# One stage for the sample's attention and the output projection of a two-branch encoder layer

## The reference, cut to what matters

```python
def mixer_layer(x, c, pos, past_sb_k, past_sb_v, past_ckv, past_krope, ...):
    h = rms_norm(x, pre_g) * (1.0 + scale) + shift
    sb_q, sb_k, sb_v, sb_g, c_q, c_kv, k_rope, mla_g = split_cols(h @ w_in, IN_SIZES)
    ...
    sb_o = sweep_query_blocks(stick_breaking_block, (sb_q,), (all_sb_k, all_sb_v), pos, k_pos)
    mla_o = sweep_query_blocks(mla_block, (q_nope, q_rope), (k_nope, all_krope, mla_v), pos, k_pos)
    mixed = jnp.concatenate([sb_o.reshape(b, t, SB_WIDTH) * jax.nn.silu(sb_g),
                             mla_o.reshape(b, t, MLA_WIDTH) * jax.nn.silu(mla_g)], axis=-1)
    y = x + gate * rms_norm(mixed @ w_out, post_g)
```

## Time and profile before

| what | value |
|---|---|
| device time, 3 runs | 2635.29, 2643.12, 2650.52 us; median 2643.12 |
| profiled execution | 2648.48 us device time; span 2646.7 us from first to last instruction |
| busy shares of the span | PE 85%, PEld 71%, DVE 52%, ACT 50%, POOL 29% |
| granted TensorE clock, mean | 0.917 of full |
| prompt attention | ends at 2088 us |
| sample attention and output | 2091.6 to 2646.7 us |
| transfers from 2090 us on | 81.08 MB in 100408 packets, mean 146 GB/s |

### The profile page before, as it was taken

How to read it: one execution, slowest core, us unless ns; L and a number is a source line. 1 busy time by engine, 2 the same in 40 slices (tenths; PEclk the granted TensorE clock), 3 DMA queues, 4 the chain that set the end, 5 groups by cost and what they waited for, 6 DMA issues and landing times. The chain is left out here.

```text
span 2646.7 us, 40141 instructions
## 1 busy us (share of the span) xinstructions
PE 2248.5 (85%) x12099; PEld 1869.0 (71%) x12099; DVE 1381.5 (52%) x2759; ACT 1323.5 (50%) x2852; POOL 776.9 (29%) x773
## 2 busy tenths in 40 slices
PE   6599996999977899498989999999989577775887
PEld 1488885899967677286868677777778356664765
DVE  2223232210137333487878778787878388863332
ACT  1223222211112433388888888888888555542221
POOL 0000000000000000356474737465563345542321
PEclk9799998899989899699999999999999777777989
DMA  8333322222337898733323343332320444426773
GB/s 292 106 101 95 108 83 89 100 80 82 116 92 198 284 310 290 158 67 69 68 66 75 70 91 67 68 82 58 74 54 23 107 136 135 142 67 196 177 185 93
DMA packets 304695, 314.44 MB, mean 119 GB/s; under 512 B 88322, under 2 KB 234765, under 8 KB 299489
## 3 DMA queue, kind: packets, MB, share of 16 engines
q1 hardware_dynamic: 299810, 297.45, 40.9%
q10 hardware_dynamic: 3744, 12.19, 1.2%
q0 software_dynamic: 992, 3.21, 0.3%
HBM read 194.83 MB, written 109.57 MB: 115 GB/s over the span
## 5 line engine op out<-in xcount | busy, mean ns | idle before, releaser
L1243 ACT ACTIVATE pa_whi<-banks 128x512 fp32r<-128x512 f32 (+3 forms) x640 | 346.4, 542 | 98.9 <-PE banks L1468 77.9
L1468 PE MATMUL banks<-ident,pa_p 128*128 128x128 f32 x2176 | 354.9, 279 | 2.2 <-ACT pa_p L1208 2.2
L1451 PE MATMUL banks<-pa_khi,pa_qst 128*128 128x512 f32 (+3 forms) x640 | 262.7, 410 | 103.9 <-DVE pa_p L1307 77.1
L1397 POOL TENSOR_TENSOR pa_wlo<-pa_whole,pa_whi 128x512 fp32r<-128x512 f32 (+2 forms) x240 | 279.2, 1172 | 191.4 <-ACT pa_whole L1248 190.7
L1379 POOL CAST pa_khi<-pa_kraw 128x512 fp32r<-128x512 f32 x64 | 39.1, 611 | 993.4 <-DMA pa_kraw<-scratch_sb_kT 993.4
L1468 PEld LDWEIGHTS banks<-ident,pa_p 128*128 128x128 f32 x2176 | 268.5, 143 | 61.4 <-issue 5.6
L1428 PE MATMUL banks<-pa_whi,pa_vst 128*128 128x512 f32 (+3 forms) x640 | 285.1, 445 | 1.5 <-POOL pa_wlo L1397 1.4
L1307 DVE TENSOR_TENSOR_SCAN pa_p<-banks,pa_p,pa_zero 128x512 f32<-128x512 f32 x192 | 246.3, 1283 | 71.4 <-ACT banks L1201 62.6
L1451 PEld LDWEIGHTS banks<-pa_khi,pa_qst 128*128 128x128 f32 x640 | 125.7, 196 | 184.2 <-DVE pa_p L1307 142.7
L1284 DVE TENSOR_TENSOR pa_wlo<-banks,pa_whi 128x512 fp32r<-128x512 f32 (+3 forms) x400 | 234.7, 587 | 27.0 <-ACT pa_whi L1243 27.0
L1452 PE MATMUL banks<-pa_klo,pa_qst 128*128 128x512 f32 (+3 forms) x640 | 242.6, 379 | 0.0
(11 more groups left out here) (231 smaller groups left out, 5095.6 us busy)
## 6 DMA issues: line engine op xcount, KB each, us to landing
ada<-in_ada_w_dram SPq DMA_DIRECT2D x6, 2048.0 KB, 11.4
scratch_sb_kT<-ke_kT SPq DMA_DIRECT2D x12, 1024.0 KB, 8.9
scratch_mla_kT<-ke_nT SPq DMA_DIRECT2D x12, 1024.0 KB, 5.5
scratch_mla_v<-ke_v SPq DMA_DIRECT2D x12, 1024.0 KB, 5.4
co_hlo<-scratch_hT SPq DMA_DIRECT2D x6, 1408.0 KB, 6.9
scratch_gatesT<-co_gates SPq DMA_DIRECT2D x12, 704.0 KB, 10.7
pr_x<-in_x_prompt_dram SPq DMA_DIRECT2D x16, 512.0 KB, 4.4
scratch_hT<-pr_hT SPq DMA_DIRECT2D x16, 512.0 KB, 5.3
```

Source lines behind the costliest of these rows:

```text
L1243: act.activation(whi[:, t % NW, q0:], bank, ACT.Copy).then_inc(hi_done, 1)
L1397: pool.tensor_tensor(wlo[:, t % NW, q0:], whole[:, t % 4, q0:], raw(whi[:, t % NW, q0:]), ALU.subtract).then_inc(pool_lo, 1)
L1451: pe.matmul(bank, qst[job][:, q], khi[job][:, keys], start=True, stop=False)
L1468: y = pe.transpose(ps[:, NS + t % NTB, x * P:(x + 1) * P], probs[g][x][:, i * P:(i + 1) * P], s["ident"][:])
```

## The change

`sample_attention_phase` and `output_phase` are replaced by one function, `tail_phase`, with one table of slots. Slot t (from -11 to 78) does: score chunk t + 10, transpose and take out chunk t, one quarter of an output tile (12 matmuls: half of the 8 contraction chunks for one half of the 1024 columns), and mix chunk t - 1. 72 chunks and 64 quarters; quarter i is put into slot i * 8 // 7, so slots 7, 15, ... 71 have none. Each engine has a list per slot. The 16 prompt tiles are projected this way; the sample's own tile keeps its gated, split operands in SBUF (`shi`, `slo`) and is projected at the end (`sample_part`, 42 matmuls in slot 72 and 6 after the last job).

Operands are held in rings: keys `klo` (3 chunks, split in place, with 2 of `khi`), rotary keys `krst` (3), values (3), weights (3). A key chunk is loaded when the chunk three before it has been scored. Scores of a stick-breaking job stay in PSUM: the sigmoid is in place there, and the scan reads PSUM and writes `left`. The copy that makes the high part of the values moves from ACT and DVE to POOL for all chunks. The exponentials of a softmax job are issued in three pieces of three chunks (slots 9J - 1, 9J + 1, 9J + 4). The output's square is taken per half tile, PSUM for the output has three banks. `w_out` comes through a ring of three buffers (the tiles `x` and `y`) during slots -10 to -3; its low part is made by DVE and POOL in turn.

The keys stage now stores the rotary keys split: DVE writes `krhi` and `krlo` (one more 32-row subtraction per tile), SP issues three transfers per group in place of one; prompt attention loads the 96 rows in one transfer without splitting them.

```diff
@@ keys_phase
-                    sp.dma_start(d["mla_krT"][:, at], krT[:, b, 0:n]).then_inc(krT_stored[b], 16)
+                    for i, tile in enumerate((krhi, krhi, krlo)):
+                        sp.dma_start(d["mla_krT"][i * ROPE:(i + 1) * ROPE, at], raw(tile[:, b, 0:n])).then_inc(krT_stored[b], 16)
...
-                        dve.tensor_copy(krT[:, b, at], ps[0:ROPE, 2 + j % 2, RC * P:RC * P + rows])
+                        rope = ps[0:ROPE, 2 + j % 2, RC * P:RC * P + rows]
+                        dve.tensor_copy(krhi[:, b, at], rope).then_inc(kr_hi, 1)
...
+                        dve.wait_ge(kr_hi, NT * g + j + 1)
+                        dve.tensor_tensor(krlo[:, b, at], rope, raw(krhi[:, b, at]), ALU.subtract).then_inc(c_ev, 1)
@@ prompt_attention_phase
-                for i in range(3):
-                    sp.dma_start(early[i * ROPE:(i + 1) * ROPE, 0:T], d["mla_krT"][:, 0:T]).then_inc(kr_loaded, 16)
+                sp.dma_start(raw(krst[:]), d["mla_krT"][:, 0:T]).then_inc(kr_loaded, 16)
...
-                act.activation(krst[:], early[0:3 * ROPE, 0:T], ACT.Copy).then_inc(kr_hi, 1)
...
-                dve.tensor_tensor(krst[lo, :], early[lo, 0:T], raw(krst[lo, :]), ALU.subtract).then_inc(const_done, 1)
@@ tail_phase
+    AHEAD = 10
+    RING = 3
+    FIRST_SLOT, END_SLOT = -AHEAD - 1, U + 7
...
+        def quarter_slot(i):
+            return i * 8 // 7
+        def tile_slot(n):
+            return quarter_slot(4 * n)
+        def half_slot(n, i):
+            return quarter_slot(4 * n + 2 * i + 1)
...
+                def load_k(u):
...
+                    if u >= RING:
+                        sp.wait_ge(scores, u - RING + 1)
...
+                    for n in tiles:
+                        if t == tile_slot(n) - 7:
+                            load_tile(n)
+                        if t == tile_slot(n) + 2:
+                            load_x(n)
+                        if t == half_slot(n, 1) + 3:
+                            store(n)
...
+            @block.scalar
+                for t in slots:
...
+                    if 0 <= t + AHEAD < U and not is_soft(t + AHEAD):
+                        sigmoid(t + AHEAD)
+                    for n in tiles:
+                        for i in range(2):
+                            if t == half_slot(n, i) + 1:
+                                square(n, i)
+                    if 0 <= t < U:
+                        high(t)
+                    if 0 <= t + AHEAD + 1 < U:
+                        split_k(t + AHEAD + 1)
+                    for J in range(1, JOBS, 2):
+                        for at, pieces in ((-1, (0, 1, 2)), (1, (3, 4, 5)), (4, (6, 7, 8))):
+                            if t == NCH * J + at:
+                                for k in pieces:
+                                    exp(NCH * J + k)
...
+                        if t == half_slot(n, 1) + 1:
+                            root(n)
...
+            @block.vector
+                    if 0 <= u < U:
+                        if is_soft(u):
+                            cut(u)
+                        else:
+                            scan(u)
+                    if 0 <= t < U:
+                        low(t)
...
+                    if 0 <= u + 1 < U:
+                        split_k(u + 1)
...
+            @block.tensor
+                def score(u):
...
+                    pe.wait_ge(k_split, u + 1)
...
+                    if u >= 2:
+                        pe.wait_ge(cut_done if is_soft(u - 2) else scan_done, nth(u - 2) + 1)
...
+                for t in slots:
+                    if 0 <= t + AHEAD < U:
+                        score(t + AHEAD)
+                    if 0 <= t < U:
+                        turn(t)
...
+                    for i in range(4 * TILES):
+                        if t == quarter_slot(i):
+                            quarter(*divmod(i, 4))
+                    if 0 <= t - 1 < U:
+                        mix(t - 1)
```

More of the change, by code:

```diff
@@ new lines, in tail_phase @@
+        scores, sig_done, scan_done, taken_done = sm.one("scores"), sm.one("sig"), sm.one("scan"), sm.one("taken")
+        cut_done, negtop_done, exp_done = sm.one("cut"), sm.one("negtop"), sm.one("exp")
+        total_done, inverse_done = sm.one("total"), sm.one("inverse")
+        turned, hi_done, lo_done, mix_done = sm.one("turned"), sm.one("hi"), sm.one("lo"), sm.one("mix")
+        half_done, summed, divided, gated, shi_done, slo_done = (
+            sm.one(n) for n in ("half", "summed", "divided", "gated", "shi", "slo"))
@@ L1599, in sample_attention_phase, with columns @@
+        def columns(i):
+            return slice(i * CH, (i + 1) * CH)
+        slots = range(FIRST_SLOT, END_SLOT)
+        tiles = range(TILES)
         with nc.Block() as block:
@@ L1819, in finish, with take_inverse @@
+                def take_inverse(J):
+                    e = entry(NCH * J + NCH - 1) + 1
+                    dve.wait_ge(turned, e + 1)
+                    if J > 1:
+                        dve.wait_ge(divided, J // 2)
                     for hd in range(2):
                         part = slice(hd * HD, (hd + 1) * HD)
[L1821 to L1823 removed]
@@ L1838, in _, with finish @@
-                jobs_in_turn(dve, split=split, step=step, chunk=chunk, finish=finish, late=late)
+                        r = dve.tensor_copy(inverse_rows[part, :], ps[part, 2 + e % 2, hd * Q:(hd + 1) * Q])
+                    r.then_inc(lo_done, 1)
+                def finish(J):
+                    dve.wait_ge(half_done, J + 1)
+                    if J:
+                        dve.wait_ge(slo_done, J)
+                    for hd in range(2):
+                        part = slice(hd * HD, (hd + 1) * HD)
+                        a = dve.tensor_tensor(mine[part, :], ps[part, SUMS, hd * Q:(hd + 1) * Q], half[part, :], ALU.add)
+                    a.then_inc(summed, 1)
@@ new lines, in difference @@
+                def difference(u):
+                    keys, i = keys_of(u), nth(u)
+                    n = keys.stop - keys.start
+                    pool.wait_ge(scan_done, i + 1)
+                    if i >= RING:
+                        before = i - RING
+                        pool.wait_ge(turned, entry(2 * NCH * (before // NCH) + before % NCH) + 1)
+                    pool.tensor_tensor(taken[:, i % RING, 0:n], left[:, keys.start + 1:keys.stop + 1], left[:, keys],
+                                       ALU.subtract).then_inc(taken_done, 1)
@@ new lines, in _ @@
+                for t in slots:
+                    if 0 <= t + 2 < U and not is_soft(t + 2):
+                        difference(t + 2)
+                    if 0 <= t + 1 < U:
+                        split_v(t + 1)
+                    for J in range(JOBS):
+                        if t == NCH * J + 10:
+                            finish(J)
+                    u = t + AHEAD
+                    if 0 <= u < DC and u % 2:
+                        split_w(u)
+                    for n in tiles:
+                        if t == tile_slot(n) - 4:
+                            gate_tile(n)
@@ new lines, in turn @@
+                def turn(u):
+                    e, i, keys = entry(u), nth(u), keys_of(u)
+                    n, rows = blocks_of(u)
+                    pe.wait_ge(exp_done if is_soft(u) else taken_done, i + 1)
+                    if e >= 2:
+                        pe.wait_ge(lo_done, e - 1)
+                    weights = soft[:, keys] if is_soft(u) else taken[:, i % RING, :]
+                    for j in range(n):
+                        y_ = pe.transpose(ps[0:rows, 2 + e % 2, j * P:(j + 1) * P], weights[:, j * P:j * P + rows], s["ident"][:])
+                    y_.then_inc(turned, 1)
@@ new lines, in turn_inverse, with mix @@
+                def turn_inverse(J):
+                    e = entry(NCH * J + NCH - 1) + 1
+                    pe.wait_ge(inverse_done, J // 2 + 1)
+                    pe.wait_ge(lo_done, e - 1)
+                    pe.transpose(ps[:, 2 + e % 2, 0:P], inverse[:].to_broadcast([P, P]), s["ident"][:]).then_inc(turned, 1)
+                def mix(u):
+                    J, k = divmod(u, NCH)
+                    n, rows = blocks_of(u)
+                    r = u % RING
+                    pe.wait_ge(lo_done, entry(u) + 1)
+                    pe.wait_ge(v_split, u + 1)
+                    if k == 0 and J:
+                        pe.wait_ge(summed, J)
+                    for j in range(n):
+                        pe.matmul(ps[:, SUMS, 0:2 * P], vhi[0:rows, r, j, :], w[0:rows, r, j].rearrange("p a q -> p (a q)"),
+                                  start=(k == 0 and j == 0), stop=False)
+                        mm = pe.matmul(ps[:, SUMS, 0:P], vlo[0:rows, r, j, :], w[0:rows, r, j, 0, :],
+                                       start=False, stop=(k == NCH - 1 and j == n - 1))
+                    mm.then_inc(mix_done, 1)
@@ new lines, in quarter @@
+                def quarter(n, q):
```

(14 more changed lines are left out.)

863 lines of the change are left out of this document (399 added, 464 removed).

## The result

The changed kernel took **2563.8 us** (median of 4 runs, 2560.8 to 2564.5) beside 2641.8 us before (4 runs, 2635.3 to 2650.5): 0.970 of it, 95% interval 0.9671 to 0.973. Forecast were 2540 us, 0.961 of the time before. Its profiled execution took 2564.2 us and has a span of 2562.4 us. The sum of the prediction ended at 2544.6 us of span, so it is 17.8 us short.

What follows compares the result with a forecast made beforehand. Attention left PE idle, the projection needed mostly PE, and nearly 60 us went into entries. 2091.6 + entry 40 + slots 392 + end 21 gave 2544.6 us of span, said as 2540 us; range 2480 to 2605.

Steps and rivals of the forecast that it cites:

- Entry, 40 us: Start of the merged stage: rotary split gone, `w_out` loads added, ten chunks prepared; 40 us, bounds 30 and 50.
- the ring of engines: Stick-breaking slots: scores, sigmoid, scan, keys' low part; 4.3 us without handovers, 4.9 taken, nearly hidden under PE's 4.75.
- Slots on PE, 4.98 and 4.75 us: PE time of a slot with a quarter: 4.98 us with softmax scores, 4.75 with stick-breaking scores.
- Exponentials 20, roots 6: ScalarE in the slots: nine exponential pieces delay 20 us, bounds 0 and 40; roots in seven stick-breaking slots cost 6.
- Late loads 16: Slots: tile transfers queue ahead of a chunk's keys, mostly hidden; 1 us per tile, 16 in all, bounds 0 and 48.
- Clock 22: Slots: 20 gaps that drop PE's clock, 1.1 us each; 22 us, bounds 0 and 45.
- Slots in all, 392: All slots: PE sum 328, exponentials 20, roots 6, clock 22, late loads 16; 392 us.
- Rival "transfers bound the stage": Merged stage: 322 us of transfer work at 0.64 engine share; about 2600 us, from 2580 to 2630, chance 0.18.
- Rival "TensorE at the low level": Slots: handover gaps hold the clock at 1.2 GHz; 2815 us in all, slower than before, chance 0.06.
- Rival "near PE's floor", 2490: Merged stage: lists absorb pieces and loads, no clock lost; 2479 us, 2490 with a little of each, chance 0.13.
- The upper bound 2605: Range's top: half of each upper bound together (slots 450, entry 46, end 22), or the transfers' case at its middle.
- The signs: Right: slots 5.3 to 5.5 us, clock over 0.9, first quarter some 40 us in. Wrong: ACT or POOL awaiting loads.

Runs made afterwards that it cites:

- experiment 1: Changed kernel with the next chunk's keys split ahead of the sigmoid on ScalarE and ahead of the scan on VectorE: 2559.5 us.
- experiment 7: Changed kernel with tile loads spread over slots, plus quarters starting in slot 4 and `w_out` split four slots later: 2530.3 us.
- Experiment 8: Changed kernel with spread tile loads, keys split first, quarters from slot 4 and `w_out` split four slots later: 2498.1 us.
- experiments 2 and 3: Changed kernel, once with the roots as copies: 2555.2 us; once with the exponentials as sigmoids: 2550.7 us.
- experiments 4 and 5: Changed kernel, once with tile loads cut to a fraction of their bytes: 2533.4 us; once with the same bytes spread over slots: 2533.5 us.
- experiment 6: Changed kernel with tile loads spread over slots and the next chunk's keys split ahead of sigmoid and scan: 2517.9 us.
- experiment 9: Kernel before with only the rotary keys' part: split in the keys stage, loaded ready by both attentions: 2625.5 us beside 2644.2.

## Why the prediction was right, and where its terms were off

Direction and range held, and so did the mechanism: the projection's matmuls fill attention's gaps, both entries go. The time saved is 78 us where 103 were forecast. By its own steps:

- **Entry, 40 us: 53.0 measured, above its bound of 50. This is the term that was mis-sized most**, 13 of the 17.8 us. The estimate scaled the ten chunks of the kernel before, which came every 2.56 us, and kept the ring of engines for the slots alone. But the ring (scores, sigmoid, scan, keys' low part) has nothing to hide behind in the priming, and there a chunk takes 4.22 us. Only the text's "4.3 without handovers" was needed, ten times, with 8.7 us ahead of it. The late `w_out`, which the text named for its bound, is the second cause: with the ring taken out alone the priming still took 41.1 us (experiment 1), and with `w_out` moved alone it ran at 4.22 us a chunk (experiment 7). Experiment 8 takes both causes away and has 29.8 us.
- **Slots on PE, 4.98 and 4.75 us:** 5.08 and 4.73. **The ring hides under them** in undisturbed slots, as said. Slots without a quarter saved nothing: where the text took 5 us off for four of them (its own 2.72 us a quarter would make 11, without a reason given for the rest), the softmax ones (7, 23, 39, 55) took 4.4, 6.5, 5.3 and 7.0 us, TensorE waiting 1.9 to 5.1 us at the end of each.
- **Exponentials 20, roots 6:** the table loads alone are 13 and 8.5 us by experiments 2 and 3. Right in size. The Trainium skill (ScalarE: Activation LUTs, What ACT_TABLE_LOAD costs) counts a drain of about 1.38 us on top of each load. In the rows the sigmoid follows 0.02 us behind the load, and no run lost more than 0.8 us per load, so the measurement decides against adding it here.
- **Late loads 16: mis-sized, 30 measured** (experiments 4 and 5), within its bounds of 0 and 48. The text took 1 us per tile and a cover of 10 to 15 us for a chunk's keys. It did not put store, `x`, mixed, gates and inverse into one slot, though the issue order says so, nor the time that SyncE spends on issuing when much is under way, nor that the tile's own operands could be late.
- **Clock 22:** the granted clock was 0.91. The 768 quarter matmuls sum to 321.7 us (rows L2123: 112.2, with 105.0 and 104.5 for the other two products of the same line), and at the 0.39 of the earlier trace rows they would be 299.5, so 22 us for the quarters. Right in size. By the text's own formula for the projection (time at the low level, half of it lost) 0.91 over 395.4 us would be 36 us, but that counts as lost also what TensorE only waited at the low level.
- **Slots in all, 392: 395.4.** Late loads were 14 us dearer than taken, and the sum was still right within 3.4. The terms are not independent (the 30 us of spreading hold a part of the clock's, which rose from 0.91 to 0.94): a piece of exponentials, a late chunk and a fallen clock meet in the same slot and are paid once. That the sum holds is partly luck.
- **End 21:** 22.4. **Keys and prompt stages 0:** 0 at the prompt's first matmul (1088.81 beside 1089.06 us), 1 at the new stage's.
- **Rival "transfers bound the stage":** the slots did run at a share of 0.66, close to its 0.64, and the time came out between the forecast and it. But the share was no limit: 0.76 in experiment 6, 0.80 in experiment 8. What was true of it was the queue's order, not the bytes.
- **Rival "TensorE at the low level":** no. Undisturbed slots are at full clock, low levels follow waits, as behind the 5.33 us at 2411.38, where the matmul takes 0.79 us. The page of the Trainium skill that it named (TensorE: Matmul & The Clock Gate, A second HAM failure mode) describes swings between groups of matmuls, and the trace has both levels within the slots: 0.91 in the mean. That is nowhere near enough to turn the sign.
- **Rival "near PE's floor", 2490:** not this kernel, but its order can be mended to 2498.
- **The upper bound 2605:** half of each upper bound together gives slots of some 436 us, not 450 (6.8 for the ring, 10 for exponentials, 11.5 for the clock, 16 for late loads on top of 392), an entry of 45 and a time near 2591. The range rests on the transfers' case, then.
- **The signs:** the mean slot of 5.49 us and the clock of 0.91 came; the first quarter came 53 us after the entry, not some 40. One of the signs of being wrong came in part: ScalarE waited 35.6 us for the tiles and 20.1 for keys. The longest wait for the keys' low part, 5.33 us, lies in a slot with a piece of exponentials as forecast, but what held it up was the keys' transfer.

## What to carry to other kernels

When two stages are merged, list per slot what each queue issues, in order, and look for the slot in which a whole tile's transfers stand ahead of the next small operand; spreading them cost nothing here and gave 30 us. Price a dependency ring twice, once beside the work that hides it and once in the priming where nothing does. And when an edit that should work brings 4 us, look at what is waited for now before dropping it: the same edit brought 15.6 once the transfers were spread, and late quarters, worth 3 alone, came with 20 at the end. When a part is timed by itself, look in the windows for where its gain lies: 17 of experiment 9's 24 us lay in a stage that the edit does not touch.

## What was not expected of the hardware

Issuing a transfer took SyncE 0.43 us in the median for one load of values, but 2.47 us for the one at 2403.73, behind a burst; a load of the inverse (rows of 512 bytes) took 1.67 us in the median in the changed kernel and 0.62 in the spread one. So a burst delays the queue's later issues as well as their transfers.

A VectorE scan that reads PSUM took 1.28 us in every kernel with the new stage, as forecast, also beside a busy POOL, where the scan between SBUF tiles in the kernel before took 1.91. What was not expected is that the slow scan is not slow by its tiles alone. In the priming of the kernel before:

```profile
2114.60 1.27 DVE L1778 TENSOR_TENSOR_SCAN sa_row<-sa_row,sa_zero 128x512 f32<-128x512 f32 x1
...
2118.94 2.05 DVE L1778 TENSOR_TENSOR_SCAN sa_row<-sa_row,sa_zero 128x512 f32<-128x512 f32 x1
```

```profile
2118.51 1.40 POOL L1852 TENSOR_TENSOR sa_p<-sa_row 128x512 f32<-128x512 f32 x1 [1.16 <-DVE sa_row L1778]
```

The first scan runs while POOL is idle and takes 1.27 us out of SBUF, the second beside POOL's subtraction and takes 2.05.
